# A two-layer encoder on one core: the next layer's parameter rows issued by SyncE between weight tiles, and an output that leaves in eight transfers

## The chip, the core and the metric

One NeuronCore of a Trainium2 chip. The metric is the device time in microseconds (us) of one launch, here of the only core in use. Lower is better. Engines are written PE (TensorE), DVE (VectorE), ACT (ScalarE), POOL (GpSimd) and SP (SyncE). ACTq and SPq stand for the part of ACT and SP that issues DMA transfers.

## The reference

The kernel computes two layers of an encoder on 512 tokens of width 1024, in float32. Cut to what matters:

```python
def hybrid_layer(x, pos, ...):
    h = rms_norm(x, norm1_g)
    a_q, a_k, a_v, b_q, b_k, b_v, c_qkv, d_cq, d_ckv, d_kr, gates = split(h @ w_in)
    oa = windowed_gqa(...)             # A, 8 heads
    ob = differential_attention(...)   # B, 4 heads x 2 maps
    oc = dilated_attention(...)        # C, three dilations
    od = latent_attention(...)         # D
    merged = sum(sigmoid(gates_i) * (o_i @ w_branch[i]) for the four)
    x = x + merged @ w_o
    u = depthwise_conv(rms_norm(x, norm2_g) @ ffn_w_up, ffn_conv_w, ffn_conv_b)
    g, up = split(u)
    return x + (silu(g) * up) @ ffn_w_down

def reference(x, positions, ...):      # for both layers, each with its own weights
    x = hybrid_layer(x, pos, ...)
```

Besides its weight matrices each layer has small parameters: the gains of the norms, the convolution's weights and bias. They are what the change's "parameter rows" hold.

## The kernel before, in words

**Layers.** `with layers(engine) as l` is a loop of two turns on every engine. Its body is one layer, written out in a fixed order for each engine. `ORDER` gives the dense products (`C0q` ... `down2b`) and a number of steps for each; `START` and `END` are their places on one common count of steps, and `WINDOW` says in which steps each attention runs. Several generators (dense products, turns, attentions, splits) name a place for each of their pieces, and `together` merges them by place. So the order on an engine is fixed when the program is built; each piece then waits on the semaphores of what it needs, and an engine never passes a waiting instruction.

**Dense products.** A weight tile is two chunks of 128 rows by 512 columns (512 KB). SP loads it into one of the two halves of `raw` (line 453), once the tile two before it has been split (the wait at line 450). ACT copies `raw` to the rounded high part `wh` (line 844, in `split_next`), DVE subtracts to get the low part `wl` (line 1296). Both have three slots, so ACT also waits until PE has finished with the tile three before. PE then runs 24 matmuls for a tile (line 504): four banks, two chunks, three products of high and low parts. ACT takes the finished banks out of PSUM; for a gate that is `gates_out` (line 892, a Tanh), and DVE's `branch_out` or `add_to_x` (line 1467) does it for products that go to the sum or to `x_sb`.

**Attention B** runs beside the products from `br0a` to `gate1b`. For each of its 32 units PE computes scores (line 748), DVE adds the bias (1758), ACT takes the exponential (1183), DVE mixes two maps (1746), PE turns the mix (534), ACT and DVE copy the two halves of the turned mix out of PSUM (1177 and 1752), and PE multiplies by the values (739). After each group of heads DVE scales the result (1767) and frees PE's accumulator `O1`.

**Parameter rows.** `parameter_rows(layer)` yields 16 small loads into the tile `rows`: two norm gains, `cq`, `ckv`, `subln`, six head-norm gains that are read twice over, `dq`, `dk`, and three pieces of 88 or 44 rows with the convolution's weights and bias. Those of layer 0 are loaded at the start, six by ACT and ten by SP. Those of the next layer are issued by ACT in `dense()` (lines 962 and 963), in a row, between `gates_out("gate0b")` and `gates_out("gate1a")`. PE turns `rows` at the start of each layer, after a wait on `params_in`. In the second layer the same 16 loads are issued again, of layer 0's rows; nobody reads them, but ACT waits for them at its end.

**Output.** `x_sb` holds x as four tiles of 128 tokens by 1024 features. The last products, `down2a` and `down2b`, add to its left and right 512 columns, four token tiles each (line 1467). After the last of these eight additions SP stores all of `x_sb` with one transfer of 2048 KB (line 456) and waits for it.

Of the kernel before, what the change touches and what calls it, by code (L numbers as in the profile page):

```python
# [21 lines left out]
P = 128  # L22
DM, SEQ, DEPTH = 1024, 512, 2
TT = SEQ // P
# [3 lines left out]
BW = 512  # L28
# [78 lines left out]
class Own:  # L107
# [12 lines left out]
    pj_dve=108, sq_used=60, normed=53, combined=4, sublayer_normed=4, h_normed=8, td_ready=69, td_act=69, td_dve=69, nt_ready=16, nt_act=16,  # L120
# [17 lines left out]
START, END = {}, {}  # L138
# [64 lines left out]
def _build(nc, io, ctx):  # L203
# [5 lines left out]
    def signal(name, before=0, unit=1):  # L209
        s = Signal(ctx.enter_context(nc.semaphore(name)), before, EACH.get(name, 0), unit)  # L210
        signals[name] = s
        return s

    def sem(name):
        return ctx.enter_context(nc.semaphore(name))
# [28 lines left out]
    def in_work(at, n, **dims):  # L244

        names = " ".join(dims)
        return work[:, at:at + n].rearrange(f"p ({names} n) -> p {names} n", **dims)
# [15 lines left out]
    x_sb, h_sb = in_work(AD, 4096, t=4), in_work(AD + 4096, 4096, t=4)  # L263
# [34 lines left out]
    pj_dve = signal("pj_dve", before=8)  # L298
# [37 lines left out]
    params_in = signal("params_in", before=16, unit=16)  # L336
# [10 lines left out]
    out_done = sem("out_done")  # L347
# [6 lines left out]
    def layers(eng):  # L354
        return eng.Fori(0, DEPTH)


    def weight_tiles(l):
        def chunk_rows(w, kt, chunks=2):
            return w[bass.ds(l, 1), kt * P * chunks:(kt + 1) * P * chunks, :].rearrange("a (c p) n -> p (a c) n", p=P)  # L360

        w_in, w_up, w_down = io["w_in"], io["ffn_w_up"], io["ffn_w_down"]
        w_br = io["w_branch"].rearrange("l b k n -> l (b k) n")

        def block(w, *cols, kts=range(4)):
            for kt in kts:
                at, pieces = 0, []
                for c0, n in cols:
                    pieces.append((at, n, chunk_rows(w, kt)[:, :, c0:c0 + n]))
                    at += n  # L370
                yield pieces, 2, at, kt == kts[-1]

        def of(name):
            half = "ab".find(name[-1])
            if name[0] == "C":
                yield from block(w_in, (COL["C"] + (3 * int(name[1]) + "qkv".find(name[2])) * BW, BW))
            elif name == "kv":
                yield from block(w_in, (COL["Akv"], 256), (COL["ckv"], KVR))
            elif name == "cq":
                yield from block(w_in, (COL["cq"], QR), (COL["kr"], ROPE))  # L380
            elif name[:4] == "gate":
                yield from block(w_in, (COL["gate"] + int(name[4]) * DM + half * BW, BW))
            elif name[:2] == "br":
                yield from block(w_br, (half * BW, BW), kts=range(2 * int(name[2]), 2 * int(name[2]) + 2))
            elif name[:2] == "dq":
                cols = slice(int(name[2]) * 384, int(name[2]) * 384 + 384)
                yield [(0, 384, chunk_rows(io["d_w_uq"], 0)[:, :, cols])], 2, 384, False
                yield [(0, 384, chunk_rows(io["d_w_uq"], 2, 1)[:, :, cols])], 1, 384, True
            elif name[:2] == "dk":
                yield from block(io["d_w_ukv"], (int(name[2]) * BW, BW), kts=range(1))  # L390
            elif name == "Aq":
                yield from block(w_in, (COL["Aq"], BW))
            elif name[0] == "B":
                yield from block(w_in, (COL["B"] + "qkv".find(name[1]) * BW, BW))
            elif name[0] == "o":
                yield from block(io["w_o"], (int(name[1]) * BW, BW))
            elif name[:2] == "up":
                b = int(name[2:])
                yield from block(w_up, (256 * b, 256), (FF + 256 * b, 256))
            elif name[:4] == "down":  # L400
                g = int(name[4])
                first = sum(UP_GROUPS[:g])
                yield from block(w_down, (half * BW, BW), kts=range(first, first + UP_GROUPS[g]))

        for name, _steps in ORDER:
            for i, tile in enumerate(of(name)):
                yield START[name] + 4 * i, tile

    def parameter_rows(layer):

        at = bass.ds(layer, 1)
        for name, key in (("norm1_g", "norm1"), ("norm2_g", "norm2"), ("d_cq_norm", "cq"), ("d_ckv_norm", "ckv"),
                          ("b_subln_g", "subln")):
            src = io[name][at].rearrange("a (r c) -> (a r) c", c=P)
            yield rows[ROW[key]:ROW[key] + src.shape[0], 0, :], src
        for name, key in (("a_q_norm", "aq"), ("a_k_norm", "ak"), ("b_q_norm", "bq"), ("b_k_norm", "bk"),
                          ("c_q_norm", "cqn"), ("c_k_norm", "ckn")):
            yield (rows[ROW[key]:ROW[key] + 1, 0, :].rearrange("p (a n) -> p a n", a=2),
                   io[name][at, :].unsqueeze(1).to_broadcast([1, 2, HD]))
        yield rows[ROW["dq"]:ROW["dq"] + 1, 0, 0:NOPE], io["d_q_norm"][at, 0:NOPE]  # L420
        yield rows[ROW["dk"]:ROW["dk"] + 1, 0, 0:NOPE], io["d_k_norm"][at, 0:NOPE]
        conv_w = io["ffn_conv_w"][at].rearrange("a k (r c) -> (a k r) c", c=P)
        yield rows[0:88, 1, :], conv_w[0:88, :]
        yield rows[0:44, 2, :], conv_w[88:132, :]
        yield rows[44:88, 2, :], io["ffn_conv_b"][at].rearrange("a (r c) -> (a r) c", c=P)
# [8 lines left out]
    @block_.sync  # L434
    def _(sp):
        for dst, src in ((work[:, 512:1024].bitcast(I32), io["positions"][0, :].partition_broadcast(P)),
                         (work[:, 256:260].bitcast(I32), io["positions"].rearrange("a (t p) -> p (a t)", p=P)),
                         (work[:, 260:264].bitcast(I32), io["positions"].rearrange("a (p r) -> p (a r)", r=RES)),
                         (consts[:], io["k_consts"])):
            sp.dma_start(dst, src, allow_slow_non_contiguous=True).then_inc(small_in, 16)  # L440
        sp.dma_start(x_sb, io["x"].rearrange("a (t p) n -> p (a t) n", p=P)).then_inc(x_in, 16)
        sp.wait_ge(rows_clear, 1)
        for dst, src in list(parameter_rows(0))[6:]:
            sp.dma_start(dst, src, allow_slow_non_contiguous=True).then_inc(params_in.handle, params_in.unit)
        for dst, src in ((near[:], io["k_near"]), (work[:, 0:256].rearrange("p (m n) -> p m n", m=2), io["k_mask_c12"])):
            sp.dma_start(dst, src).then_inc(setup_in, 16)
        with layers(sp) as l:
            for k, (_when, (pieces, chunks, cols, _last)) in enumerate(weight_tiles(l)):

                sp.wait_ge(*tile_split.at(l, k - 1))  # L450
                dst = raw[:, k % 2, 0:chunks * cols].rearrange("p (c n) -> p c n", c=chunks)
                for at, n, src in pieces:
                    sp.dma_start(dst[:, :, at:at + n], src).then_inc(*(raw_landed[k % 2]).up())

        sp.wait_ge(*pj_dve.at(DEPTH, 0))
        sp.dma_start(io["y"].rearrange("a (t p) n -> p (a t) n", p=P), x_sb).then_inc(out_done, 16)
        sp.wait_ge(out_done, 16)


    @block_.gpsimd  # L460
# [342 lines left out]
    def _(act):  # L803
        a = nc.scalar.activation
# [18 lines left out]
        with layers(act) as l:  # L823
# [60 lines left out]
            def gates_out(name, dst, after):  # L884

                for m in range(4):
                    yield END[name] - 2.7 + m
                    if m == 0 and after is not None:
                        act.wait_ge(*after)
                    src = ready()  # L890
                    act.wait_ge(*own.done(l))
                    a(dst[m], src[:, :], ACT.Tanh, scale=0.5).then_inc(*pj_act.up(own))
# [29 lines left out]
            def dense():  # L922
# [36 lines left out]
                yield from values_out("Bv", vB)  # L959
                n_ready[0] += 4  # L960
                yield from gates_out("gate0b", GATES, merged_sum.at(l, 12))
                for dst, src in parameter_rows((DEPTH - 1) - l):
                    act.dma_start(dst, src, allow_slow_non_contiguous=True).then_inc(*params_in.up())  # L963
                n_ready[0] += 4
                yield from gates_out("gate1a", GATES, merged_sum.at(l, 16))
                yield from gates_out("gate1b", SPARE, None)
# [13 lines left out]
                for g, size in enumerate(UP_GROUPS):  # L980
                    for i in range(size):
                        end = END[f"up{b}"]
                        for m in range(4):
                            yield end - 2.7 + m
                            src = ready()
# [20 lines left out]
            def group():  # L1006

                n_turn[0] += 1
                act.wait_ge(*td_ready.at(l, n_turn[0]))
                return TD  # L1010
# [207 lines left out]
            src = group()  # L1218
# [647 lines left out]
```

## Time and profile before

| | |
|---|---|
| median of 3 runs | 2839.29 us (2838.62 to 2845.24) |
| the profiled execution's own time | 2839.23 us |
| its span in the trace | 2837.4 us |
| busy: PE, DVE, ACT | 94%, 55%, 43% of the span |
| mean granted TensorE clock | 0.984 of full speed |
| chain that ended last | PE 77%, DVE 10%, issue 6%, ACT 5%, ACTq 1% |

The profiled execution is 1.8 us longer than its span: what lies before the first and after the last traced instruction. A row of the timeline gives the start, the length, the engine, the line, the operation, what it writes and reads, and in brackets how long the engine had been idle and what ended that. DMA-issuing instructions are not counted as busy, so time in which ACT issues transfers shows up as idle time of ACT with the releaser "issue", and as ACTq rows.

### The profile page before, as it was taken

How to read it: one execution, taken by the hardware profiler on the slowest of the kernel's cores; microseconds unless marked ns; L12 is line 12 of the kernel's file. 1: busy time of each engine (PE TensorE's matmuls, PEld its weight loads, DVE VectorE, ACT ScalarE, POOL GpSimd, SP SyncE). 2: the span in 40 equal slices, each digit the busy share in tenths (PEclk: the TensorE clock that was granted, in tenths of full speed). 3: DMA queues.
4: the chain of work that ended last, by engine and by line, in shares of the span. 5: the costliest groups of instructions: out<-in, count | busy, mean ns of one | idle time of the engine just before them, and what ended most of it. 6: DMA issues, size and time to landing. Idle time of an engine off the chain costs nothing.

```text
span 2837.4 us, 44319 instructions
## 1 busy us (share of the span) xinstructions
PE 2665.1 (94%) x12974; PEld 2226.9 (78%) x12974; DVE 1563.7 (55%) x3226; ACT 1221.8 (43%) x2487; POOL 1.5 (0%) x6
## 2 busy tenths in 40 slices
PE   5999989999998989999979999899999989899998
PEld 4899977777776768888869998777777757788887
DVE  5454476544465556564655545765355556465745
ACT  4455544344543334242445555534445433343422
POOL 0000000000000000000000000000000000000000
PEclk9999999999999999999999999999999999999999
DMA  5212213222121322333332122221221213233332
GB/s 161 75 53 83 78 47 95 62 68 75 53 69 46 104 75 90 98 98 98 94 105 75 46 83 77 69 83 53 67 81 56 67 39 112 75 97 97 96 97 91
DMA packets 143546, 225.98 MB, mean 80 GB/s; under 512 B 14969, under 2 KB 69579, under 8 KB 142411
## 3 DMA queue, kind: packets, MB, share of 16 engines
q1 hardware_dynamic: 132585, 200.62, 23.4%
q10 hardware_dynamic: 10722, 22.45, 2.3%
q8 instruction: 116, 1.90, 0.3%
q14 instruction: 123, 1.01, 0.1%
HBM read 210.39 MB, written 12.65 MB: 79 GB/s over the span
## 4 chain that ended last, share of the span: by engine, by line
PE 77%; DVE 10%; issue 6%; ACT 5%; ACTq 1%; DVEq 1%; SPq 0%; DMA 0%
PE bank L504 60%; PE bank L704 5%; PE bank L534 5%; PE bank L694 5%; DVE s_wl L1296 2%; PE bank L748 1%; ACT s_wh L844 1%; PE bank L739 1%; DVE s_gTl L1629 1%; DVE s_work L1455 1%; ACTq L963 1%; PE bank L570 1%; ACT s_gTh L1025 1%; ACT s_work L1114 0%; DVE s_work L1396 0%
## 5 line engine op out<-in xcount | busy, mean ns | idle before, releaser
L1296 DVE TENSOR_TENSOR s_wl<-s_raw,s_wh 128x1024 fp32r<-128x1024 f32 (+2 forms) x376 | 453.9, 1208 | 430.3 <-ACT s_wh L844 427.5
L844 ACT ACTIVATE s_wh<-s_raw 128x1024 fp32r<-128x1024 f32 (+2 forms) x376 | 392.4, 1044 | 517.6 <-PE bank L504 464.5
L504 PE MATMUL bank<-s_hTh,s_wh 128*128 128x512 f32 x1216 | 525.6, 432 | 6.7 <-DVE s_work L1393 6.7
L504 PE MATMUL bank<-s_hTh,s_wl 128*128 128x512 f32 x1216 | 478.6, 394 | 0.0
L504 PE MATMUL bank<-s_hTl,s_wh 128*128 128x512 f32 x1216 | 478.3, 393 | 0.0
L504 PE MATMUL bank<-s_wh,s_hTh 128*128 128x512 f32 (+1 forms) x1088 | 469.5, 432 | 4.7 <-DVE s_early L1393 4.7
L504 PE MATMUL bank<-s_wh,s_hTl 128*128 128x512 f32 (+1 forms) x1088 | 426.7, 392 | 0.0
L504 PE MATMUL bank<-s_wl,s_hTh 128*128 128x512 f32 (+1 forms) x1088 | 425.6, 391 | 0.0
L504 PEld LDWEIGHTS bank<-s_hTh,s_wh 128*128 128x128 f32 x1216 | 231.4, 190 | 75.3 <-issue 23.9
L504 PEld LDWEIGHTS bank<-s_hTl,s_wh 128*128 128x128 f32 x1216 | 231.7, 191 | 67.5 <-issue 24.4
L1114 ACT ACTIVATE s_work<-s_work,s_stat 128x128 f32<-128x128 f32 (+3 forms) x320 | 167.4, 524 | 269.1 <-DVE s_work L1788 118.6
L504 PEld LDWEIGHTS bank<-s_wh,s_hTh 128*128 128x128 f32 x1088 | 252.1, 232 | 38.0 <-DVE s_early L1393 6.4
L504 PEld LDWEIGHTS bank<-s_wl,s_hTh 128*128 128x128 f32 x1088 | 253.8, 233 | 27.7 <-issue 0.5
L504 PEld LDWEIGHTS bank<-s_wh,s_hTl 128*128 128x128 f32 x1088 | 251.8, 231 | 27.0
L504 PEld LDWEIGHTS bank<-s_hTh,s_wl 128*128 128x128 f32 x1216 | 231.0, 190 | 49.8
L534 PE MATMUL bank<-s_consts,s_work 128*128 128x128 f32 (+1 forms) x1432 | 219.2, 274 | 42.2 <-DVE s_gTl L1629 24.2
L534 PEld LDWEIGHTS bank<-s_consts,s_work 128*128 128x128 f32 (+1 forms) x1432 | 172.7, 139 | 99.9 <-DVE s_gTl L1629 33.4
L1713 DVE COPY s_work<-bank 128x128 f32<-128x128 f32 (+1 forms) x224 | 77.8, 347 | 270.5 <-ACT s_work L1102 202.1
L504 PE MATMUL bank<-s_wh,s_gTh 128*128 128x512 f32 (+1 forms) x432 | 165.9, 384 | 0.0
L504 PE MATMUL bank<-s_wh,s_gTl 128*128 128x512 f32 (+1 forms) x432 | 165.5, 383 | 0.0
L504 PE MATMUL bank<-s_wl,s_gTh 128*128 128x512 f32 (+1 forms) x432 | 165.4, 383 | 0.0
L1102 ACT ACTIVATE s_work<-bank 128x256 f32<-128x256 f32 (+1 forms) x224 | 78.5, 350 | 113.0 <-PE bank L534 112.0
(184 smaller groups left out, 3363.7 us busy)
## 6 DMA issues: line engine op xcount, KB each, us to landing
s_raw<-in_w_in SPq DMA_DIRECT2D x168, 512.0 KB, 3.6
s_raw<-in_ffn_w_up SPq DMA_DIRECT2D x176, 256.0 KB, 2.9
s_raw<-in_ffn_w_down SPq DMA_DIRECT2D x44, 512.0 KB, 3.6
s_raw<-in_w_branch SPq DMA_DIRECT2D x32, 512.0 KB, 3.6
s_raw<-in_w_o SPq DMA_DIRECT2D x16, 512.0 KB, 3.7
x_keep<-s_work ACTq DMA_DIRECT2D x2, 2048.0 KB, 7.2
s_raw<-in_w_in SPq DMA_DIRECT2D x16, 256.0 KB, 3.0
gate_keep<-s_early ACTq DMA_DIRECT2D x4, 1024.0 KB, 4.4
```

Source lines behind the costliest of these rows:

```text
L504: last = mm(PJ[b][:, 0:width], st, mv, start=i == 0 and n == 1, stop=i == ntiles - 1 and n == 3 * chunks)
L534: last = nc.tensor.transpose(dst[0:m, (at + n) * P:(at + n) * P + k], src, ident[0:k, 0:k])
L570: last = nc.tensor.transpose(dst[:, t * P:t * P + P], h_sb[:, t, P * c:P * c + P], ident)
L694: last = mm(out, st, mv, start=start, stop=stop)
L704: last = mm(out, st, mv, start=True, stop=True)
L739: last = mm(O1[:, P * h:P * h + P], probsT[:, pair % 2, P * k:P * k + P], vB[:, k, P * h:P * h + P], start=k == 0, stop=k == 3)
L748: mm(out, st, mv, start=True, stop=True).then_inc(*s_ready.up())
L844: a(wh[:, k % 3, 0:n], raw[:, s, 0:n], ACT.Copy).then_inc(*hi_split.up(own))
L1102: a(probsT[:, u % 2, P * lo:P * mid], src[:, P * lo:P * mid], ACT.Copy).then_inc(*ta_act.up(own))
L1114: a(probs[:, u % 2, x0:x0 + w], scores[:, u % 2, x0:x0 + w], ACT.Exp, scale=-1.0, bias=stat[:, mins, c:c + 1], accum_out=stat[:, sums, c:c ...
L1296: v.tensor_tensor(wl[:, k % 3, 0:n], raw[:, k % 2, 0:n], wh[:, k % 3, 0:n].bitcast(F32), ALU.subtract).then_inc(*tile_split.up(own))
L1713: v.tensor_copy(probsT[:, u % 2, P * mid:P * hi], src[:, P * mid:P * hi]).then_inc(*ta_dve.up(own))
```

## The change

SP's loop over weight tiles now keeps an iterator over the 16 parameter rows of the next layer. After each weight tile from `gate1a` on it issues one row, until the 16 are out: four with `gate1a`, four with `gate1b`, two each with `br1a` and `br1b`, four with `o0`. ACT's 16 issues between `gate0b` and `gate1a` are gone. At the end SP waits for each of the eight additions to `x_sb` in turn and stores that block, 128 tokens by 512 columns, 256 KB; then it waits for all eight.

```diff
         with layers(sp) as l:
-            for k, (_when, (pieces, chunks, cols, _last)) in enumerate(weight_tiles(l)):
+            next_rows = parameter_rows((DEPTH - 1) - l)
+            for k, (when, (pieces, chunks, cols, _last)) in enumerate(weight_tiles(l)):
 
                 sp.wait_ge(*tile_split.at(l, k - 1))
                 dst = raw[:, k % 2, 0:chunks * cols].rearrange("p (c n) -> p c n", c=chunks)
                 for at, n, src in pieces:
                     sp.dma_start(dst[:, :, at:at + n], src).then_inc(*(raw_landed[k % 2]).up())
-
-        sp.wait_ge(*pj_dve.at(DEPTH, 0))
-        sp.dma_start(io["y"].rearrange("a (t p) n -> p (a t) n", p=P), x_sb).then_inc(out_done, 16)
-        sp.wait_ge(out_done, 16)
+                row = next(next_rows, None) if when >= START["gate1a"] else None
+                if row is not None:
+                    sp.dma_start(*row, allow_slow_non_contiguous=True).then_inc(*params_in.up())
+
+        y = io["y"].rearrange("a (t p) n -> p (a t) n", p=P)
+        for cb in range(2):
+            for t in range(TT):
+                sp.wait_ge(*pj_dve.at(DEPTH, 4 * cb + t + 1 - 8))
+                sp.dma_start(y[:, t, BW * cb:BW * cb + BW], x_sb[:, t, BW * cb:BW * cb + BW]).then_inc(out_done, 16)
+        sp.wait_ge(out_done, 16 * 8)
...
                 yield from gates_out("gate0b", GATES, merged_sum.at(l, 12))
-                for dst, src in parameter_rows((DEPTH - 1) - l):
-                    act.dma_start(dst, src, allow_slow_non_contiguous=True).then_inc(*params_in.up())
                 n_ready[0] += 4
                 yield from gates_out("gate1a", GATES, merged_sum.at(l, 16))
```

In the lists below a row is a line of the kernel, the operation (ISA is a wait, an addition to a semaphore or register work), what is written and read, and the shape. In the changed kernel the lines after the edit in SP's part are numbered up to 7 higher, and those after the edit in ACT's part 5 higher.

ACT, from the last evacuation of `gate0b` to the first high-part copy and the first copy of B's turned mix behind it, before:

```order
L892 ACTIVATE s_work<-bank 128x512
L963 ISA
L963 DMA s_rows<-in_norm_g 8x128
...
L963 ISA
L963 DMA s_rows<-in_a_q_norm 1x2x64
...
L963 ISA
L963 DMA s_rows<-in_ffn_conv_b 44x128
L841 ISA
L843 ISA
L844 ACTIVATE s_wh<-s_raw 128x1024
L1087 ISA
```

and SP at the first weight tiles of `gate1a`, with the change:

```order
L454 DMA s_raw<-in_w_in 128x2x512
L457 ISA
L457 DMA s_rows<-in_norm_g 8x128
L451 ISA
L454 ISA
L454 DMA s_raw<-in_w_in 128x2x512
L457 ISA
L457 DMA s_rows<-in_norm_g 8x128
```

The 16 DMA rows that stood together on ACT stand one by one on SP, each behind a weight tile and ahead of the next tile's wait (L451).

SP's last rows, before:

```order
L453 DMA s_raw<-in_ffn_w_down 128x2x512
L447 REGISTER_ALU
L447 COMPARE_AND_BRANCH
L456 DMA out_y<-s_work 128x4x1024
L159 UNCONDITIONAL_BRANCH
```

and with the change:

```order
L454 DMA s_raw<-in_ffn_w_down 128x2x512
L447 REGISTER_ALU
L447 COMPARE_AND_BRANCH
L463 DMA out_y<-s_work 128x512 x8
L159 UNCONDITIONAL_BRANCH
```

One store of four token tiles by 1024 columns has become eight stores of one token tile by 512 columns, each behind its own wait.

## Rows read from the trace of the kernel before

**Rows 1.** The page, part 1: busy time, share of the span, instructions

```profile
PE 2665.1 (94%) x12974; PEld 2226.9 (78%) x12974; DVE 1563.7 (55%) x3226; ACT 1221.8 (43%) x2487; POOL 1.5 (0%) x6
```

**Rows 2.** Who waited for whom on PE: us in total, times, longest

```profile
PE bank L739 <- DVE s_work L1767: 22.2, 2, 11.1
```

**Rows 3.** Timeline of layer 0 around ACT's 16 issues

```profile
888.66 0.60 ACT L892 ACTIVATE s_work<-bank 128x512 f32<-128x512 f32 x1
...
891.32 0.39 PE L504 MATMUL bank<-s_gTh,s_wl 128*128 128x512 f32 x1
891.42 0.72 ACTq L963 DMA_DIRECT2D s_rows<-in_a_q_norm  x1
...
899.33 1.06 ACT L844 ACTIVATE s_wh<-s_raw 128x1024 fp32r<-128x1024 f32 x1 [10.06 <-issue]
...
900.78 0.42 DVE L1752 COPY s_work<-bank 128x256 f32<-128x256 f32 x1 [13.08 <-ACT s_work L1177]
...
902.84 2.08 PE L739 MATMUL bank<-s_work 128*128 128x128 f32 x8 [11.13 <-DVE s_work L1767]
```

**Rows 4.** Timeline of layer 1, the same place

```profile
2302.61 1.06 ACT L844 ACTIVATE s_wh<-s_raw 128x1024 fp32r<-128x1024 f32 x1 [10.04 <-issue]
...
2306.12 2.08 PE L739 MATMUL bank<-s_work 128*128 128x128 f32 x8 [11.10 <-DVE s_work L1767]
```

**Rows 5.** Stretches: length, each engine's busy us, PEclk, DMA share, GB/s

```profile
902.50:905.50 3.00, 2.67 (x9) 2.21 (x10) 2.55 (x5) 0.27 (x2) 0.00 (x0) 0.50 0.15 19
905.50:906.00 0.50, 0.50 (x3) 0.34 (x1) 0.00 (x0) 0.00 (x0) 0.00 (x0) 0.60 0.64 152
...
2306.00:2312.00 6.00, 5.88 (x16) 4.36 (x17) 3.03 (x7) 1.02 (x4) 0.00 (x0) 0.50 0.30 87
2312.00:2312.50 0.50, 0.50 (x5) 0.32 (x4) 0.00 (x0) 0.47 (x2) 0.00 (x0) 0.81 0.00 0
```

**Rows 6.** Who waited for whom on SP: us in total, times, longest

```profile
SPq L453 <- DVE s_wl L1296: 2494.2, 373, 23.3
```

**Rows 7.** Timeline at SP's closest pair of weight tiles in `o0`, layer 0

```profile
1002.02 1.51 SPq L453 DMA_DIRECT2D s_raw<-in_w_o  x2
...
1010.74 1.04 ACT L844 ACTIVATE s_wh<-s_raw 128x1024 fp32r<-128x1024 f32 x1
```

**Rows 8.** Timeline at the end of attention B, layer 1

```profile
2357.32 0.37 SPq L453 DMA_DIRECT2D s_raw<-in_w_in  x1
...
2366.35 1.06 ACT L844 ACTIVATE s_wh<-s_raw 128x1024 fp32r<-128x1024 f32 x1 [4.22 <-DMA s_raw<-in_w_in]
2368.53 1.23 DVE L1296 TENSOR_TENSOR s_wl<-s_raw,s_wh 128x1024 fp32r<-128x1024 f32 x1
```

**Rows 9.** Timeline at the start: a parameter row and PE's wait

```profile
8.13 0.35 SPq L444 DMA_DIRECT2D s_rows<-in_ffn_conv_b  x1
...
13.28 0.90 PE L534 MATMUL bank<-s_consts,s_rows 128*128 128x128 f32 x3 [13.28 <-DMA s_rows<-in_ffn_conv_b]
```

**Rows 10.** Timeline of the last additions to `x_sb` and the store

```profile
2825.64 0.69 DVE L1467 TENSOR_TENSOR s_work<-bank,s_work 128x512 f32<-128x512 f32 x1 [10.02 <-PE bank L504]
...
2829.72 0.69 DVE L1467 TENSOR_TENSOR s_work<-bank,s_work 128x512 f32<-128x512 f32 x1 [0.67 <-PE bank L504]
2830.44 0.40 SPq L456 DMA_DIRECT2D out_y<-s_work  x1
```

**Rows 11.** DMA issues: count, KB each, median us from issue to landing

```profile
s_raw<-in_ffn_w_up SPq DMA_DIRECT2D x176, 256.0 KB, 2.9
...
s_raw<-in_w_o SPq DMA_DIRECT2D x16, 512.0 KB, 3.7
...
gate_keep<-s_early ACTq DMA_DIRECT2D x4, 1024.0 KB, 4.4
...
out_y<-s_work SPq DMA_DIRECT2D x1, 2048.0 KB, 6.6
...
s_raw<-in_d_w_uq SPq DMA_DIRECT2D x4, 192.0 KB, 2.3
```

## The prediction

> **What bounds the kernel now.** I read the page first: PE is busy for 94% of the span [rows 1]. An edit that takes no matmul away can therefore pay only where PE stands still, where it runs at a lower clock, or after its last matmul. So the next view is who PE waited for, and there one row belongs to this change: PE line 739 waited 22.2 us for DVE line 1767, in only two waits, the longer of 11.1 us [rows 2]. There are two layers, so this is once a layer.
>
> The timeline around it shows why [rows 3]. ACT's last Tanh of `gate0b` ends at 888.66 + 0.60 = 889.26. Then ACT issues the 16 parameter rows, and its next compute instruction, the high-part copy at line 844, starts at 899.33. The bracket says that it waited 10.06 us for "issue", so for nothing but ACT's own sequencer. Behind it on ACT stands line 1177, the copy of attention B's turned mix, and DVE line 1752 waits for that (13.08 us idle). DVE then does a few short pieces up to line 1767, and PE line 739, which needs that, starts at 902.84 after 11.13 us of idleness. PE's last matmul ahead of it ended at 891.71. In layer 1 the same rows read 10.04 and 11.10 us [rows 4].
>
> The clock has to be read at the same place. When PE comes back its granted clock is 0.50, that is 1.2 GHz instead of 2.4, after the 11 us without work. It stays there for all of 902.50 to 905.50 and for part of the next half microsecond; in layer 1 for 2306 to 2312 and a little more [rows 5].
>
> The end comes last: the final addition is done at 2830.41, SP issues the store at 2830.44 [rows 10], and the 2048 KB land 6.6 us later [rows 11]. No engine works in that time.
>
> **The change part by part.**
>
> *ACT without its 16 issues.* What goes is the idle time before line 844, less the 0.04 us that lies between two instructions anyway: 10.0 us in each layer. It comes off PE in full only if nothing else is late. Line 844 copies the first tile of `gate1a`. SP issues a tile when the one two before has been split, which for this one was long before the gap, so it lies in `raw`. Its slot was last used by `gate0b`, whose last bank ACT had just evacuated. Line 1177 needs B's turned mix, and PE's last matmul before the gap ended at 891.71. DVE was idle. The latest thing that ACT could still wait for is PE's work up to 891.71; that would put line 844 at 891.75 and make the gain 7.6 us. I take 10.0 and keep 7.6 as the lower bound; above 10.0 there is nothing to remove. PE's gap becomes 11.1 - 10.0 = 1.1 us. Two layers: **-20.0 us** (bound -15.2).
>
> *The clock.* If PE waits only 1.1 us there I expect no fall. A half microsecond at 0.60 is 0.4 us at 0.50 and 0.1 at 1.00, so PE worked at half clock from 902.84 to 905.90, 3.06 us; in layer 1, by the same reading, from 2306.12 to 2312.19, 6.07 us [rows 5]. At full clock this work takes half as long: 1.5 + 3.0 = **-4.5 us**. Bounds: 0, if the clock falls anyway, and 4.5. Other stretches of low clock stand elsewhere in the trace (the mean is 0.984). The two layers show that the same program text can spend 3.0 us more or less at half clock, which is 1.5 us of time; for two such places I allow 3 us either way.
>
> *SP with 16 more issues a layer.* On ACT 16 issues took 10.06 us, 0.63 us each (the longest instruction is 0.72 [rows 3]); on SP the same, in 16 pieces. They stand behind a weight tile and ahead of SP's next wait. SP waited 2494.2 us for DVE in 373 waits [rows 6], 6.7 us a tile, so a piece of under 1 us fits. The closest tiles of the stretch are two of `o0`, both issued within 1.51 us of 1002.02 [rows 7]. The row between them may move the second from about 1003.2 by less than 1 us. A tile of 512 KB lands in 3.7 us [rows 11], so the first is there at 1005.7, and ACT copies it only at 1010.74 and the second after that: 5.0 us of slack. The tightest landing is that of the tile of 2357.32: it comes while ACT's reload of x (2048 KB) is under way, and ACT waits 4.22 us for it [rows 8]. The row ahead of it leaves with the tile before, some 5 us earlier, and is out of the way; even so DVE splits this tile only at 2368.53, 1.1 us after ACT's copy ended (2367.41). I cost SP's pieces at **0**. PE needs the rows only at the start of the next layer, hundreds of us later.
>
> A rule speaks against this part. The row shows that issuing cost ACT 10.06 us of its place in line and PE nearly all of that [rows 3]. The Trainium skill (DMA: Bandwidth & Descriptors, section Issuing engines are not separate DMA queues) says that issuing from several engines saves only the sequencer's time, "which is usually small relative to the DMA itself". By that rule the part is worth next to nothing and the sum is rival D's, 2835.3 us; the trace disagrees, since here the sequencer's time is itself on PE's path.
>
> *The output in eight.* The first seven blocks leave while PE still works, the last four are 1.36 us apart (2825.64 to 2829.72 in three steps [rows 10]). Only the last block's 256 KB is exposed. No store of that size is in the trace. Two stores are, 1024 KB in 4.4 us and 2048 KB in 6.6 [rows 11]: 2.2 us for each 1024 KB, which by a straight line is 4.4 - 0.75 x 2.2 = 2.75 us. The nearest loads are 192 KB in 2.3 us and 256 KB in 2.9 (of a pair, so partly behind its partner). I take 2.7, from the stores, since the direction is the same, and keep 2.3 to 2.9. Gain 6.6 - 2.7 = **-3.9 us** (3.7 to 4.3).
>
> The same page (section Anatomy of one DMA) gives a fixed cost of about 2.0 us and 436 bytes per ns for transfers issued by GpSimd; as an estimate that makes 2.6 us for 256 KB. No run here has shown such a store yet.
>
> *Sum*, on the profiled execution's 2839.23 us (the median of the runs, 2839.29, is the same): 2839.2 - 20.0 - 4.5 - 3.9 = **2810.8 us**, 1.0% faster.
>
> **The rivals.**
>
> *A, only part of the gap closes.* Another wait ends last at the same place, or work lost there was slack that returns later. For it: all engines stood, so I see no second latecomer. Against: nothing in the layer runs by an outside clock; weight loads wait for DVE, and DVE for PE, so what follows moves up as a whole. With half of the 24.5 us: 2839.2 - 12.3 - 3.9 = 2823.0.
>
> *B, the small stores queue.* If each of the eight is served to the end before the next starts, the last four, from about 2826.4 on and 2.7 us each, end at 2837.2, where the single store ended at 2837.0. The tail gains nothing: 2839.2 - 24.5 = 2814.7. For it: a store's time at these sizes is mostly not bytes (2.2 us remain at zero bytes by the line above). Against: many packets are in flight in one store, so I see no reason for a full stop between two.
>
> *C, slower.* A parameter row holds up the weight tile behind it in SP's queue. The price is bounded by the start of the program: a row issued at 8.13 released PE at 13.28, 5.15 us later, behind other loads [rows 9]. At 2.3 us, the smallest landing listed [rows 11], 32 rows cost 73.6 us: 2810.8 + 73.6 = 2884.4. It ends slower than 2839.3 by 0.3% from (28.4 + 8.5) / 32 = 1.2 us a row that no slack covers. Against: the tiles have 5 us and more of slack [rows 7], and a row has several us to finish before the next tile leaves.
>
> *D, the middle does nothing.* If the wait "issue" stands for something that moves with line 844, the gap stays, and only the tail is gained: 2835.3, within 0.3%.
>
> **How the numbers follow.** About 0.3% (8.5 us) is what a measurement of this kernel can tell from no change. The forecast gets 0.78, A 0.10, B 0.07, D 0.03, C 0.02. Faster by over 0.3% (below 2830.8) are the forecast, A and B: 0.95; same 0.03; slower 0.02. The best sum is 2810.8 less 0.4 for the tail and 3 for other clock stretches, with a little beyond: 2806. On the other side the lower bound of the gap (+4.8), the clock that falls anyway (+4.5) and B (+3.9) each give 2814.7 to 2815.6 alone; two of them together, or one with 3 us of clock elsewhere, reach 2820. A lies outside. The range is 2806 to 2820.
>
> **What would show it.** In the changed profile: ACT line 851 right behind the Tanh of `gate0b`, with no "issue" of 10 us; PE's wait of line 746 on DVE line 1772 gone from 22.2 us to about 2; clock 1.00 through the start of `br0b`'s second tile; SP rows of `s_rows` one per tile; no new ACT waits for `s_raw` in `gate1a` to `o0`; the last store landing in about 2.7 us. Wrong would be a PE gap of several us at that place, a clock of 0.50 there, or weight tiles landing late.

## The result, and the profile after

| | before | changed |
|---|---|---|
| median | 2840.72 us (4 runs, 2838.62 to 2845.24) | 2811.91 us (4 runs, 2807.87 to 2813.40) |
| ratio, 95% interval | | 0.9891 (0.9876 to 0.9906) |
| profiled execution, span | 2839.23, 2837.4 us | 2807.87, 2806.1 us |
| mean granted clock | 0.984 | 0.990 |

The changed kernel is 1.1% faster. The forecast of 2810.8 us is 1.1 us off. The runs of one kernel scatter over 5 to 7 us, so that the two agree this closely is partly luck.

The place of the gap in layer 0, timeline of the changed kernel. Line 899 is the Tanh that was line 892, 851 the high-part copy, 746 the matmuls that PE waited in front of; these rows answer to [rows 3].

```profile
886.26 0.60 ACT L899 ACTIVATE s_work<-bank 128x512 f32<-128x512 f32 x1
886.75 1.05 ACT L851 ACTIVATE s_wh<-s_raw 128x1024 fp32r<-128x1024 f32 x1
...
887.70 0.37 ACT L1182 ACTIVATE s_work<-bank 128x256 f32<-128x256 f32 x1
...
889.51 0.69 DVE L1772 TENSOR_TENSOR s_work<-bank,s_stat 128x512 f32<-128x512 f32 x1
...
890.25 1.16 PE L746 MATMUL bank<-s_work 128*128 128x128 f32 x8 [0.96 <-DVE s_work L1772]
...
891.51 0.38 SPq L454 DMA_DIRECT2D s_raw<-in_w_in  x1
...
892.14 0.28 SPq L457 DMA_DIRECT2D s_rows<-in_d_cq_norm  x1
```

The copy follows the Tanh with no gap, and PE waits 0.96 us where it waited 11.13. Layer 1 reads the same (0.96 for 11.10). The eight matmuls of line 746 take 1.16 us where they took 2.08. The two SPq rows are the change at work: a weight tile, then one parameter row.

The stretches behind it, in both layers (columns as in [rows 5]): the clock stays at 1.00, the level of 2.4 GHz.

```profile
886.00:890.00 4.00, 3.30 (x14) 2.20 (x12) 1.73 (x5) 2.66 (x6) 0.00 (x0) 1.00 0.00 0
890.00:896.00 6.00, 5.75 (x28) 4.22 (x28) 3.53 (x9) 2.23 (x7) 0.00 (x0) 1.00 0.30 88
2278.00:2282.00 4.00, 3.26 (x14) 2.17 (x12) 1.76 (x5) 2.66 (x7) 0.00 (x0) 1.00 0.00 0
2282.00:2288.00 6.00, 5.78 (x28) 4.22 (x28) 3.53 (x9) 2.19 (x7) 0.00 (x0) 1.00 0.31 88
```

The end: the last addition and, from the list of DMA issues, the store. They answer to [rows 10, 11].

```profile
2802.94 0.69 DVE L1472 TENSOR_TENSOR s_work<-bank,s_work 128x512 f32<-128x512 f32 x1 [0.67 <-PE bank L511]
```

```profile
out_y<-s_work SPq DMA_DIRECT2D x8, 256.0 KB, 2.0
```

From the last addition's end to the end of the span it was 2837.4 - 2830.41 = 7.0 us, and it is 2806.1 - 2803.63 = 2.5.

What the two places are worth in all can be read from two high-part copies, one before the gap and the third one on. In layer 0, first before, then changed:

```profile
877.40 1.04 ACT L844 ACTIVATE s_wh<-s_raw 128x1024 fp32r<-128x1024 f32 x1
...
922.60 1.06 ACT L844 ACTIVATE s_wh<-s_raw 128x1024 fp32r<-128x1024 f32 x1
```

```profile
874.99 1.04 ACT L851 ACTIVATE s_wh<-s_raw 128x1024 fp32r<-128x1024 f32 x1
...
908.58 1.06 ACT L851 ACTIVATE s_wh<-s_raw 128x1024 fp32r<-128x1024 f32 x1
```

The distance was 45.20 us and is 33.59, so 11.6 us less. Between the same copies of layer 1 it was 46.56 (2280.69 to 2327.25) and is 33.61 (2266.93 to 2300.54), 12.95 less. So the profiled spans, 31.3 us apart, divide into 24.6 us at the two places, 4.5 us at the end, and 2.2 us more. Of the 24.6 us PE's two gaps are 20.3 (11.13 + 11.10 - 2 x 0.96); the other 4.3 us are the matmuls behind the gaps, which no longer run at half clock. The 2.2 us are not the change's: 0.8 us stands ahead of the first weight tile's copy (19.12 us before, 18.30 now), where the two programs are the same, and the rest in other stretches where the clock was low in one of the two executions and not in the other.

### The profile page after: what moved, and what is told of

Same layout as the page of the kernel before. It is cut to its first block, busy times and chain, and to the rows that moved or that the text cites. A ratio compares the mean times of both kernels' runs of the same rounds, so it can differ in the third digit from the quotient of the medians.

```text
span 2806.1 us, 44326 instructions
## 1 busy us (share of the span) xinstructions
PE 2657.7 (95%) x12974; PEld 2220.3 (79%) x12974; DVE 1563.4 (56%) x3226; ACT 1221.4 (44%) x2487; POOL 1.5 (0%) x6
## 4 chain that ended last, share of the span: by engine, by line
PE 77%; DVE 11%; issue 6%; ACT 5%; DVEq 1%; ACTq 1%; DMA 0%; SPq 0%
PE bank L511 60%; PE bank L711 5%; PE bank L541 5%; PE bank L701 5%; DVE s_wl L1301 2%; PE bank L755 1%; ACT s_wh L851 1%; DVE s_gTl L1634 1%; PE bank L746 1%; DVE s_work L1460 1%; PE bank L577 1%; ACT s_gTh L1030 1%; ACT s_work L1119 1%; DVE s_work L1398 0%; DVE s_work L1401 0%
## 5 line engine op out<-in xcount | busy, mean ns | idle before, releaser
L511 PEld LDWEIGHTS bank<-s_hTl,s_wh 128*128 128x128 f32 x1216 | 231.1, 190 | 67.3 <-issue 24.6
```

The source lines that it names most:

```text
L511: last = mm(PJ[b][:, 0:width], st, mv, start=i == 0 and n == 1, stop=i == ntiles - 1 and n == 3 * chunks)
```

## The experiments

Each kernel was timed beside the kernel before on the same chip. A ratio can be set against that of the changed kernel: 0.9891 in its first measurement and 0.9895 (0.9876 to 0.9913) when it was run again, `e0_changed`, with a median of 2815.11 us beside 2844.16.

> The changed kernel again, timed beside the runs that follow, as their reference. Every theory: about 2811 us, 1.0 to 1.1% below the kernel before.

**The two parts alone.** `e1_rows_only` is the changed kernel with the old store:

```diff
-        for cb in range(2):
-            for t in range(TT):
-                sp.wait_ge(*pj_dve.at(DEPTH, 4 * cb + t + 1 - 8))
-                sp.dma_start(y[:, t, BW * cb:BW * cb + BW], x_sb[:, t, BW * cb:BW * cb + BW]).then_inc(out_done, 16)
+        sp.wait_ge(*pj_dve.at(DEPTH, 0))
+        sp.dma_start(io["y"].rearrange("a (t p) n -> p (a t) n", p=P), x_sb).then_inc(out_done, 16)
...
```

> The changed kernel with the single 2048 KB store of before; only the rows moved to SP. Theory M (two parts that add: ACT's issues stood on PE's path, 10.2 us and some half-clock time a layer, and the last store's landing, 4.5 us): about 2840.7 - 24.5 = 2816 us (2813 to 2819), PE's gap at the start of br0b's second tile about 1 us, 7.0 us between the last addition and the end of the span as before. Rival R (the parts are not independent, or the gain in the middle is mostly clock elsewhere): the time is off 2816 by more than 3 us, or the gap is gone and the time is still above 2825.

Measured: ratio 0.9911 (0.9898 to 0.9925), median 2819.81 beside 2843.62 us. `e2_stores_only` is the kernel before with the eight stores:

> The kernel before with the eight stores alone. Theory M: 2840.7 - 4.5 = about 2836 us, 2.5 us from the last addition to the end of the span, the two gaps of 11.1 us on PE unchanged. Rival Q (small stores queue one behind the other): 2840, with 7 us at the end. A gain of more than 8 us would mean that the stores do something else as well.

Measured: ratio 0.9981 (0.9972 to 0.9990), median 2838.48 us. Who PE waited for in it still has the old row, under its new line numbers:

```profile
PE bank L742 <- DVE s_work L1770: 22.2, 2, 11.1
```

and its store lands as in the changed kernel, the old one as before (first row of `e2_stores_only`, second of `e1_rows_only`, each from the list of DMA issues):

```profile
out_y<-s_work SPq DMA_DIRECT2D x8, 256.0 KB, 2.0
```

```profile
out_y<-s_work SPq DMA_DIRECT2D x1, 2048.0 KB, 6.6
```

Of 2843.6 us the ratios make 25.3 us for the rows and 5.4 us for the stores, 30.7 together; 1 - 0.9891 makes 31.0 for both at once. So the parts add, as far as intervals of some 4 us (rows) and 3 us (stores) to either side can tell. Theory M named 24.5 and 4.5. The medians themselves lie 2 to 4 us above the numbers expected, in both, and so does the kernel before on this chip (2843.62 where the expectations had started from 2840.7).

**Does it matter that SP issues, or where the issuing stands?** `e3_act_spread` takes the rows from SP and gives them back to ACT, one behind a high-part copy from `up1` on:

```diff
...
                     if k >= 3:
                         yield when - 7.6
                         split_next()
+                        row = next(next_rows, None) if when >= START["up1"] else None
+                        if row is not None:
+                            act.dma_start(*row, allow_slow_non_contiguous=True).then_inc(*params_in.up())
```

> The rows are back on ACT, but one by one, each behind a high-part copy from up1 on, where ACT waits about 4.4 us for PE before each such copy; the eight stores stay. Theory M (what counts is where the issuing stands, not which engine does it): the same as the changed kernel, about 2812 us (2809 to 2815); an ACT issue of 0.63 us comes out of ACT's waits for PE. Rival W (an issue on ACT costs its time wherever it stands): 32 x 0.63 = 20 us more, about 2832 us.

Measured: ratio 0.9899 (0.9884 to 0.9914), median 2814.21 us: the changed kernel's time. The timeline shows why.

```profile
1062.36 1.06 ACT L847 ACTIVATE s_wh<-s_raw 128x1024 fp32r<-128x1024 f32 x1 [4.38 <-PE bank L507]
1062.60 0.33 ACTq L864 DMA_DIRECT2D s_rows<-in_norm_g  x1
...
1067.80 1.06 ACT L847 ACTIVATE s_wh<-s_raw 128x1024 fp32r<-128x1024 f32 x1 [4.38 <-PE bank L507]
1068.02 0.30 ACTq L864 DMA_DIRECT2D s_rows<-in_norm_g  x1
```

ACT waits 4.38 us for PE at each of these copies, with or without the issue between them, and from 1060 to 1200 us PE is busy for 140.00 of 140.00 us in this kernel as in the changed one. Rival W is out: an issue on ACT is free where ACT waits for PE. All 32 issues are on ACT here, so the price before came from where they stood and not from the engine.

**The dose.** `e4_act_eight` leaves the first eight rows on ACT at the old place, `e10_act_four` the first four; SP has the rest. The edit for eight (for four, both `8` read `4`):

```diff
-            next_rows = parameter_rows((DEPTH - 1) - l)
+            next_rows = iter(list(parameter_rows((DEPTH - 1) - l))[8:])
...
                 yield from gates_out("gate0b", GATES, merged_sum.at(l, 12))
+                for dst, src in list(parameter_rows((DEPTH - 1) - l))[:8]:
+                    act.dma_start(dst, src, allow_slow_non_contiguous=True).then_inc(*params_in.up())
```

> Half a dose: ACT issues the first eight rows in a row at the old place, SP the other eight one by one; the eight stores stay. Those eight took ACT from 888.7 to 893.9, about 5.2 us. Theory M: PE's gap is about 1.0 + 5.2 = 6.2 us a layer, so 2812 + 10.4 = 2822 us if PE's clock holds, and 3 to 6 us more if it falls as it did in the gaps of 11 us, 3.5 and 4.0 us after PE's last matmul: 2825 to 2828. Rival T (some slack takes up the first few us): below 2818 us. Rival C (the cost is mostly the clock and does not shrink with the gap): above 2830.

> A quarter of the dose: ACT issues the first four rows at the old place, SP the other twelve. These took 888.7 to 890.7 before, about 2.0 to 2.3 us. Theory M: PE's gap is 1.0 + 2.2 = 3.2 us a layer. With gaps of 0.96, 5.8 and 11.1 us for 0, 8 and 16 rows in hand the line is straight, so 2 x 2.2 = 4.4 us more than the changed kernel if the clock holds there, 2818 to 2819, and clock 1.00 in and behind the gap; if the clock falls at the place, some 2 us more a layer. Rival T (the first issues are free): as the changed kernel, gap 1.0.

Measured: eight, ratio 0.9946 (0.9933 to 0.9960), median 2827.35 us; four, 0.9922 (0.9909 to 0.9936), 2819.31 beside 2842.68. Who PE waited for, first in `e4_act_eight`, then in `e10_act_four`:

```profile
PE bank L746 <- DVE s_work L1774: 11.7, 2, 5.8
```

```profile
PE bank L746 <- DVE s_work L1774: 5.5, 2, 2.7
```

The longest waits are 0.96, 2.7, 5.8 and 11.1 us for 0, 4, 8 and 16 rows on ACT, while ACT's idle time marked "issue" reads 0, 1.67, 4.75 and 10.06. Each us that ACT issues is a us of PE's gap; no first part of it is free. Rival T is out.

The times grow by more than the gaps. Eight rows cost 0.9946 - 0.9895, that is 14.5 us, with 9.8 us of gap (11.7 - 1.9); four cost 7.7 us with 3.5 us of gap. As differences of two ratios these costs are uncertain by 6 to 7 us, so the times alone do not show a surplus. The distance between the two high-part copies of the section on the result does, place by place:

| rows on ACT at the old place | layer 0, layer 1 | over the changed kernel, both | of it gap | left |
|---|---|---|---|---|
| 0 (changed; run again) | 33.59, 33.61; 33.56, 33.55 us | | | |
| 4 (`e10_act_four`) | 36.95, 36.95 us | 6.7 us | 3.5 us | 3.2 us |
| 8 (`e4_act_eight`) | 40.61, 40.18 us | 13.6 us | 9.8 us | 3.8 us |
| 16 (before) | 45.20, 46.56 us | 24.6 us | 20.3 us | 4.3 us |

The stretches behind the gap show what the last column is. First `e4_act_eight`, layer 0, PE back at 894.72; then `e10_act_four`, layer 0, PE back at 895.66, and layer 1, PE back at 2295.07:

```profile
893.00:895.00 2.00, 0.28 (x1) 0.28 (x2) 1.93 (x6) 0.81 (x2) 0.00 (x0) 0.50 0.00 0
895.00:899.00 4.00, 4.00 (x12) 2.87 (x13) 2.15 (x5) 0.00 (x0) 0.00 (x0) 0.50 0.48 126
```

```profile
892.00:896.00 4.00, 1.27 (x8) 0.76 (x7) 2.32 (x6) 2.15 (x4) 0.00 (x0) 1.00 0.00 1
896.00:898.00 2.00, 2.00 (x11) 1.48 (x9) 1.87 (x4) 0.00 (x0) 0.00 (x0) 0.61 0.05 5
898.00:900.00 2.00, 2.00 (x5) 1.19 (x5) 0.70 (x2) 0.13 (x1) 0.00 (x0) 0.54 0.86 256
...
2297.00:2299.00 2.00, 2.00 (x5) 1.22 (x4) 0.97 (x2) 0.00 (x0) 0.00 (x0) 0.50 0.79 195
```

The clock falls in both kernels, even with a gap of only 2.7 us, and there after PE had already come back. It stays low for a few us of PE's work, and half of these are lost. That is the surplus: in `e10_act_four` PE works at half clock for 3.4 us a layer, as at 896 to 900 (1.56 + 1.84), which is 1.7 us lost, 3.4 for both, against the 3.2 that are left in the table.

**SP's slack.** `e6_sp_burst_o1` lets SP issue all 16 rows in one go behind the second tile of `o1`:

```diff
-                row = next(next_rows, None) if when >= START["gate1a"] else None
-                if row is not None:
-                    sp.dma_start(*row, allow_slow_non_contiguous=True).then_inc(*params_in.up())
+                if when == START["o1"] + 4:
+                    for row in next_rows:
+                        sp.dma_start(*row, allow_slow_non_contiguous=True).then_inc(*params_in.up())
```

> SP issues all 16 rows in a row, behind the second tile of o1, where weight tiles follow each other every 5.4 us, instead of one behind each of 16 tiles. Theory M: SP is held for about 10 us, the next tile leaves some 5 us late (its wait would have ended after about 5 us) and lands about 9 us after that point; ACT copies it up to 1 us late and PE, which is two tiles behind, needs it some 4 us later still. So 0 us: as the changed kernel. Rival C (SP's queue is close to PE's path): each late us shows, 2 x 5 = 10 us more, about 2821.

Measured: ratio 0.9898 (0.9881 to 0.9914), median 2814.66 beside 2815.11 us for the changed kernel in the same job. Its timeline:

```profile
1006.87 0.86 SPq L457 DMA_DIRECT2D s_rows<-in_norm_g  x2
...
1016.57 0.29 SPq L457 DMA_DIRECT2D s_rows<-in_ffn_conv_b  x1
1017.48 1.12 SPq L454 DMA_DIRECT2D s_raw<-in_w_o  x2
1021.29 1.06 ACT L851 ACTIVATE s_wh<-s_raw 128x1024 fp32r<-128x1024 f32 x1 [6.08 <-DMA s_raw<-in_w_o]
```

SP was held for 10 us, two tiles left together, and ACT then waited 6.08 us for a tile. Its copy started 1.7 us later than in the changed kernel (1021.29 against 1016.29, where the copies before and after it lie 3.3 us apart in the two traces), and the next copy was on time again. PE did not notice: busy for 43.63 us of 990 to 1036 in this kernel and in the changed one. A burst that cost PE 10 us on ACT costs nothing on SP, since tiles are loaded about two ahead of their use. Rival C is out.

**The size of the last store.** `e7_four_stores` stores 512 KB per token tile:

```diff
-        for cb in range(2):
-            for t in range(TT):
-                sp.wait_ge(*pj_dve.at(DEPTH, 4 * cb + t + 1 - 8))
-                sp.dma_start(y[:, t, BW * cb:BW * cb + BW], x_sb[:, t, BW * cb:BW * cb + BW]).then_inc(out_done, 16)
+        for t in range(TT):
+            sp.wait_ge(*pj_dve.at(DEPTH, 4 + t + 1 - 8))
+            sp.dma_start(y[:, t, :], x_sb[:, t, :]).then_inc(out_done, 16)
...
```

> Four stores of 512 KB, one per token tile of 1024 columns, each after the right half's addition, instead of eight of 256 KB. A line through the landings measured so far (256 KB 2.0, 1024 KB 4.3, 2048 KB 6.6) gives 2.7 to 2.8 us for 512 KB. Theory M (only the last store's landing is exposed): 0.7 to 0.8 us slower than eight stores, hardly to be told in the times, but 3.2 to 3.3 us instead of 2.5 from the last addition to the end of the span. Rival Q (stores queue): 4 us or more at the end, since 1.36 us apart is then too close.

Measured: ratio 0.9899 (0.9881 to 0.9916), no difference that the times can tell. The last addition and store:

```profile
2812.26 0.69 DVE L1471 TENSOR_TENSOR s_work<-bank,s_work 128x512 f32<-128x512 f32 x1 [0.67 <-PE bank L510]
```

```profile
out_y<-s_work SPq DMA_DIRECT2D x4, 512.0 KB, 2.7
```

The span of 2816.0 us ends 3.05 us after that addition (2812.95), 0.6 more than with eight stores. Landings are 2.0, 2.7 and 6.6 us for 256, 512 and 2048 KB of output, and 4.3 for the 1024 KB of `gate_keep` in the changed kernel. Stores 1.36 us apart do not queue at either size: rival Q (B of the prediction) is out. The share of the DMA engines shows how near it is. With 256 KB it is 0.77 from 2800.4 to 2801.3 in the changed kernel and then 0.00 until 2801.7, so one store's data is through before the next one's starts; with 512 KB it is 0.96 to 1.00 from 2809.8 to 2813.5, so by an estimate from these shares larger stores at this distance would queue.

**The same reading at other gaps of PE.** ACT's squares for the norms stand between two dense products, so I tried to move them. `e8_squares_early` computes the left half's four squares for the second norm behind `o0`:

```diff
...
-                yield END["o1"]
-                squares(n_dve[0])
+                yield END["o0"] + 4.2
+                squares(n_dve[0], (0,))
+                yield END["o1"]
+                squares(n_dve[0], (1,))
```

> The changed kernel with one more step moved: the squares of the left half of x for the second norm (four ACT instructions of 0.63 us and four read-outs, 0.75 us each together) stand after o0's additions and not behind o1, where the same view shows PE idle behind ACT's eight squares. Theory M (work of ACT between two dense products is on PE's path; the same work beside a dense product is hidden): 4 x 0.75 = 3.0 us less, once a layer, so 6.0 us less than the changed kernel, about 2805, and up to 2 us beyond by the clock. Rival S (the chain behind o1's last addition sets the time, not the eight squares): the gain is only what stands ahead of that addition, 0 to 2 us a layer.

Measured: ratio 0.9894 (0.9875 to 0.9913), median 2812.34 us. Theory M's 6 us are not there. PE's wait for the scaled x before the transposes reads 15.5 us in two waits of 7.8 in the changed kernel and in this one alike. I had misread the place: in the changed kernel the squares already run beside `o1`, and the last one starts within 0.2 us of the end of the last addition. What ends last there is that addition and DVE's chain behind it.

At the start of layer 1 it looked different: the last addition ended at 1411.63, the last square at 1417.94. `e9_squares_at_start`:

```diff
...
-            split_next()
-            split_next()
-            squares(-8)
+            squares(-8, range(0, 4))
+            split_next()
+            squares(-8, range(4, 7))
+            split_next()
+            squares(-8, range(7, 8))
```

> The changed kernel with ACT's eight squares for the first norm put where their inputs are ready: four ahead of the first high-part copy of a layer, three ahead of the second, one behind it; now all eight stand behind both copies. In the trace of the changed kernel at the start of layer 1 the last addition to x ends at 1411.63 and the last read-out of a square only at 1417.94, 6.3 us later, all of it ACT's own work in line. Theory M (ACT work in line between PE's last and next matmul costs its full length): the last square would end about 0.8 us behind the second copy, 1412.7, so 5.2 us less at that place; in layer 0, where ACT only waits 1.0 us for the first tile, 1 us less. Together 6 us: about 2808 beside 2814 for the changed kernel, and PE's long wait at the start of layer 1 of 13.0 us becomes 7.8. Rival S (as at the second norm, where the same move gained nothing in the gap): something else ends last and the gap stays at 13.0.

Measured: ratio 0.9881 (0.9866 to 0.9896), median 2807.82 beside 2842.68 us, the lowest of all. Its interval overlaps the changed kernel's, so the times alone do not set them apart; the gap does. Its timeline:

```profile
1411.39 0.63 ACT L908 ACTIVATE s_work<-s_work 128x512 f32<-128x512 f32 x1
...
1413.33 1.23 DVE L1303 TENSOR_TENSOR s_wl<-s_raw,s_wh 128x1024 fp32r<-128x1024 f32 x1 [2.40 <-issue]
1414.60 0.16 DVE L1372 TENSOR_TENSOR s_stat<-s_stat 128x4 f32<-128x4 f32 x1
...
1420.73 4.52 PE L577 MATMUL bank<-s_consts,s_work 128*128 128x128 f32 x20 [10.29 <-DVE s_prm L1835]
```

The last square's read-out ends 0.8 us behind the second copy (1412.11 against 1411.36) as intended, but the gap went from 13.0 to 10.29 us only, not to 7.8. A new latecomer took over: DVE's turn of the loop (2.40 us of "issue") and its first low-part subtraction stand ahead of the norm on DVE and were hidden before. So 2.7 us were gained there of the 5.2 expected. In layer 0 PE's wait went from 19.0 to 18.3, but the kernels that leave this place alone read 18.7 to 19.9, so a gain there is not shown.

## Why the prediction was right, step by step

- *ACT's 16 issues.* Forecast 10.0 us a layer and a gap of 1.1 us that is left; it is 10.15 and 0.96. The argument that nothing else was late held, with 10.0 and not the lower bound 7.6. `e1_rows_only`, with the old store, gains it alone; `e3_act_spread` shows that the place in ACT's order was the cause and not the engine, the doses show that the price is one for one. The Trainium skill (DMA: Bandwidth & Descriptors, section Issuing engines are not separate DMA queues) calls an issue's time usually small beside the transfer; here `e1_rows_only` has 25.3 us for it, and the runs decide: what an issue costs depends on what stands behind it on its engine.
- *The clock.* Forecast 4.5 us at the two places. Measured 4.3: the two places together became 24.6 us shorter, the gaps 20.3. In `e2_stores_only`, where the middle is that of the kernel before and the gaps are the same, the two places take 25.9 us more than in the changed kernel, so this term was 5.6 there: it differs by over 1 us from one execution to the next. The clock is 1.00 there in the changed trace, and the doses show that a gap brings a loss on top of its length. That the gap would not bring the clock down at 1.1 us was an expectation for which the prediction gives no row; it held.
- *SP with 16 more issues a layer.* Forecast 0, and 5 us of slack up to ACT's copy at the closest pair of tiles in `o0`. `e6_sp_burst_o1` shows, at another pair, that even 10 us in one piece cost PE nothing, though ACT's copy was then late. Among the prediction's signs was that ACT has no new wait for `raw`. One appeared, 4.00 us at 947.44 us; but `e2_stores_only`, where SP issues no rows, has it too (4.14 us at 961.42), and it cost nothing: from the copy at 908.58 to the one at 1053.02, the stretch in which all but the first rows leave, the changed kernel takes 144.44 us, as the kernel before does from 922.60 to 1067.04.
- *The output in eight.* The one term that was mis-sized: 2.7 us for 256 KB by a straight line from 1024 and 2048 KB, measured 2.0, below the lower bound of 2.3. Gain 4.5 us instead of 3.9, above the stated bound of 4.3. A step of 256 KB costs 0.7 us from 256 to 512 KB, 0.8 up to 1024 and 0.6 up to 2048, so the two large stores gave a line with too high a foot (2.2 us at zero bytes) for the small ones. By the figures of the Trainium skill (DMA: Bandwidth & Descriptors, section Anatomy of one DMA), which are for transfers that GpSimd issues, the estimate was 2.6 us; these stores, issued by SP, landed 0.6 us sooner than that.
- *Other clock stretches.* Allowed 3 us either way. The same changed program measured 2811.91 at one time and 2815.11 at another, so this was about right.
- The rivals A to D did not occur. For D, the wait "issue" did not move with line 844 but vanished. A (part of the gap returns later) did occur elsewhere, in `e9_squares_at_start`, where another wait ended last.

On the choice of rows for the last term: the prediction says that two stores are in the trace. The list of DMA issues before has more, on ACT's queue, and these land later:

```profile
x_keep<-s_work ACTq DMA_DIRECT2D x2, 2048.0 KB, 7.2
...
c_keep<-s_early ACTq DMA_DIRECT2D x2, 1024.0 KB, 5.3
```

A line through these two gives 3.9 us for 256 KB and a gain of only 2.7. That the chosen pair came nearer was in part luck, since nothing in the prediction says why it is the right one.

## What to carry to other kernels

A DMA issue costs its engine's sequencer about 0.6 us, and 16 of them in a row on an engine that the next product depends on cost the whole kernel their full length and some clock on top; look for ACTq rows in the chain and for idle time marked "issue" in front of a copy that others wait for. Move such issues, on any engine, to where that engine waits anyway. When a wait is taken away, list what else stands in line on every engine at that place: at the `gate0b` gap there was nothing, and all 10 us came back; at the start of a layer there was a loop turn and a subtraction, and half came back (2.7 of 5.2 us).

## What the runs showed of the hardware that I had not expected

Most of the scatter of one program's time is TensorE's granted clock. Two executions of the changed kernel, measured at two times:

```profile
core 0: 2806.1 us, clock 0.990
```

```profile
core 0: 2814.9 us, clock 0.987
```

A mean of 0.990 is 56 us at half clock (2 x 0.010 x 2806), 0.987 is 73 us; half of the difference is 8.5 us, and the spans differ by 8.8. The means are rounded, so the 8.5 could as well be 6 or 11; what it shows is that the clock is large enough to be the cause. The low stretches are short and lie in different places. For instance, in the first of the two executions and then in the second:

```profile
450.00:460.00 10.00, 9.09 (x41) 7.32 (x42) 9.55 (x18) 1.06 (x1) 0.00 (x0) 1.00 0.19 55
```

```profile
450.00:460.00 10.00, 8.78 (x27) 7.05 (x28) 9.55 (x19) 0.28 (x1) 0.00 (x0) 0.66 0.26 79
```

PE does 41 matmuls in these 10 us in one and 27 in the other, with the same program and about the same idle time (0.91 and 1.22 us). And a gap of 2.7 us was enough in `e10_act_four` to bring the clock down after PE had resumed, in both layers, while with the 0.96 us of the changed kernel the clock did not fall at this place in any of the eight executions profiled that have this gap.
